# Routed expert blocks in a three-step pipeline: the down product of a block one step after the transposes of its activations, and gathers that leave out padding rows

## The chip, the cores and the metric

The kernel runs on one core of a Trainium2 chip. The core has a matrix engine (TensorE, PE in the profile), a vector engine (DVE), an activation engine (ACT), a general engine (GpSimd, POOL) and a queue engine (SyncE, SP) that here issues transfers only. The metric is the device time of one execution in microseconds; the number compared is the median of several runs.

## The reference, cut to what matters

One layer of a diffusion backbone over 1152 tokens of width 1024. The change touches the mixture of experts at its end, for which the kernel computes, with x the modulated tokens:

```python
scores = sigmoid(x @ w_router)                    # 64 experts
idx = top 8 experts of a token, limited to 4 of 8 groups
w = scores[idx] / sum * 2.5
counts = bincount(flat_e, length=64)
padded = ceil(counts / 128) * 128                 # each expert: whole blocks of 128 rows
# a block: 128 rows, all of one expert e
y_block = (silu(xb @ w_exp_gate[e]) * (xb @ w_exp_up[e])) @ w_exp_down[e]
routed = segment_sum(y_block[dest] * w_sorted, tok)
shared = (silu(x @ w_sh_gate) * (x @ w_sh_up)) @ w_sh_down
out = routed + shared
```

An expert's weights are 1024 x 256 (gate), 1024 x 256 (up) and 256 x 1024 (down) in float32, 1 MB each. How many blocks an expert has is known on the chip only, after the router; each expert has at least one.

## The kernel before, in words

**Blocks.** The expert stage works through blocks of 128 rows: blocks 0 to 8 (NT = 9) are the nine token tiles with the shared expert, blocks 9, 10, ... are the routed blocks, j = 0, 1, ... in the order of the experts. All engines run the same sequence of steps, one step for each block, written as `step(b, p, j)`, with p the parity that picks one of two buffers. The steps of the shared blocks are unrolled in Python, those of the routed blocks are a loop of the chip over pairs (`routed_steps`, L432 to L438) that ends at the block count in `endtab`.

**A block's way.** x rows come into `xg` (two buffers): for shared blocks a plain load that ACT issues (`load_rows`, L636), for routed ones an indirect gather by POOL from `hx_dram` (L583), by token numbers that DVE copies into `gidx` (L1080). PE transposes them, eight 128 x 128 (L827), ACT copies the result rounded to `xT` high (L686), and DVE subtracts to get `xT` low (L1055). Products are made in three passes of rounded parts (`products`, L792): gate/up has 24 matmuls of 512 columns, down has 12. ACT takes the SiLU of the gate half (L699), DVE multiplies with the up half (L1087) into `h_sb`. PE transposes that, two 128 x 128 (L817), ACT and DVE split it into `hTe` high (L683) and low (L1053), and PE makes the down product into banks 4 and 5. ACT copies it into `yb` (two buffers), for routed blocks times the routing weight (L717); POOL adds it into one of two `acc_dram` arrays with an indirect scatter (L602), by the numbers that DVE copies into `sidx` (L1092).

**PE's order in step b:** transposes of h(b), transposes of x(b+2), gate/up of b+1, down of b. **ACT's:** h high (b), x high (b+2), rounding of the gate/up weights of block j+2's expert if it is new (`gate_up_high`, L619, two halves), SiLU (b+1), rounding of the down weights of block j+1's expert if new (`down_high`, L624), y (b). **DVE's:** h low (b), x low (b+2), token numbers for the gather of j+4, low part of the gate/up weights of j+2's expert (`gate_up_low`, L897, two halves), gating product (b+1), numbers for the scatter of j. **POOL's:** gather j+4 (after the transposes of x(b+2)), low part of the down weights of j+1's expert (`down_low`, L565), scatter of j, which waits until the scatter two blocks before has landed.

**Weights.** SP loads an expert's raw weights into one of two slots: gate and up (L444, L445), down (L448). Its loop (from L511) is for one expert x after another: wait until gate/up of the last one have landed and tell ACT (`publish_gu`, L472), wait for `gu_low` of the expert two back, load gate/up; wait for `d_low` of the expert three back, load down; wait until the down weights before have landed and tell ACT (L476). The split weights too have two slots.

**Lists.** While the shared blocks run, the router's choice is ranked, POOL writes 72 small indirect scatters into `list_dram` (L559), block tables (`etab`, `newtab`, `endtab`) are made by small products and DVE operations placed after certain steps, and the finished lists come back over PE (`lists`, L801) ahead of the gate/up product of block 7. A padding entry of the list has the token number T + p, a row that is filled with zeros in `hx_dram` and thrown away in `acc_dram`.

## Time and profile before

| | |
|---|---|
| median of 3 runs | 1976.12 us (1967.53 to 1976.21) |
| the profiled execution | 1980.55 us |
| its span | 1978.8 us |
| PE busy | 1756.0 us (89%) |
| DVE, ACT, POOL busy | 945.0, 851.0, 774.8 us (48%, 43%, 39%) |
| shared blocks and lists | about 680 to 850 us |
| routed loop | about 850 to 1902 us |
| TensorE's granted clock, mean | 0.95 of full speed |
| moved by DMA | 425.84 MB, 215 GB/s over the span |

All rows are of one profiled execution; its own time is 1.8 us above its span. Matmuls are pipelined, so the distance between the starts of two groups says more than the busy time of one. In a row of the timeline the first number is the start, the second the time, x the number of instructions merged, and the bracket the idle time of that engine before it with what ended it. The name `arena` stands for all buffers that are cut from one large tensor.

### The profile page before, as it was taken

What the parts mean: (1) busy time and instruction counts of PE and PEld (TensorE: products, weight loads), DVE (VectorE), ACT (ScalarE), POOL (GpSimd) and SP (SyncE); (2) the same over time, 40 slices, a digit from 0 to 9 for tenths busy, and PEclk for the clock granted to TensorE, in tenths of its full rate; (3) what the DMA queues carried; (4) which work ended last, traced back from release to release, by engine and by line L of the source; (5) the groups of instructions that cost most, each with busy time, mean ns of one, the idle gap of its engine ahead of it and who ended that gap; (6) DMA issues with size and microseconds to landing.
All of it is one profiled execution on the core that took longest, in us unless ns stands there. A gap on an engine that the chain in (4) does not pass through costs nothing.

```text
span 1978.8 us, 29956 instructions
## 1 busy us (share of the span) xinstructions
PE 1756.0 (89%) x8454; PEld 1357.7 (69%) x8455; DVE 945.0 (48%) x1470; ACT 851.0 (43%) x952; POOL 774.8 (39%) x448
## 2 busy tenths in 40 slices
PE   4799999978889877789998999999999989999865
PEld 1667788868545555567777777888777767777642
DVE  5522310267466843245445455534554564445529
ACT  0521012421023431356557657634675676557623
POOL 2220000300100653256546547643564676646630
PEclk9799999987799888799999999999999999999988
DMA  9504531020552342369879989977899799879976
GB/s 330 171 19 163 173 105 35 14 86 1 194 208 91 98 174 65 113 223 343 249 234 356 299 259 355 323 197 216 265 334 286 255 363 327 292 204 345 343 227 275
DMA packets 104861, 425.84 MB, mean 215 GB/s; under 512 B 13244, under 2 KB 31801, under 8 KB 76656
## 3 DMA queue, kind: packets, MB, share of 16 engines
q1 hardware_dynamic: 62128, 279.38, 37.3%
q0 software_dynamic: 38800, 131.69, 25.6%
q10 hardware_dynamic: 3888, 14.16, 2.1%
q8 instruction: 30, 0.49, 0.1%
q14 instruction: 15, 0.12, 0.0%
HBM read 339.94 MB, written 85.25 MB: 215 GB/s over the span
## 4 chain that ended last, share of the span: by engine, by line
PE 51%; DMA 13%; DVE 12%; issue 9%; ACT 8%; another core or an unknown queue 3%; POOL 1%; ACTq 1%; DVEq 1%; SPq 0%; POOLq 0%
PE ps L792 22%; PE ps L1792 10%; DMA raw<-w_exp_up 7%; ACT gu_split L619 6%; PE ps L1923 5%; DMA arena<-hx_dram,arena 3%; PE ps L827 3%; PE ps L1740 3%; DVE gu_split L897 1%; DVE arena L1614 1%; DVE arena L1087 1%; PE ps L817 1%; DMA arena<-pos_sel 1%; PE ps L1765 1%
## 5 line engine op out<-in xcount | busy, mean ns | idle before, releaser
L792 PE MATMUL ps<-gu_split,xT 128*128 (+1 forms) x2736 | 664.3, 398 | 20.8 <-issue 20.6
L792 PEld LDWEIGHTS ps<-gu_split,xT 128*128 128x128 f32 x2736 | 511.9, 190 | 135.1 <-issue 31.6
L565 POOL TENSOR_TENSOR d_split<-raw,d_split (+1 forms) x65 | 303.8, 4674 | 248.8 <-ACT d_split L624 248.7
L792 PE MATMUL ps<-d_split,hTe 128*128 (+1 forms) x1356 | 335.4, 395 | 16.7 <-issue 12.0
L897 DVE TENSOR_TENSOR gu_split<-raw,gu_split (+1 forms) x130 | 292.6, 2292 | 87.1 <-ACT gu_split L619 80.2
L792 PEld LDWEIGHTS ps<-d_split,hTe 128*128 128x128 f32 x1356 | 258.8, 191 | 75.1 <-issue 16.8
L602 POOL DMA_INDIRECT acc_dram<-arena x104 | 202.9, 1951 | 163.5 <-ACT arena L717 143.5
L619 ACT ACTIVATE gu_split<-raw (+1 forms) x130 | 241.9, 1915 | 26.6 <-SPq L472 17.7
L1792 PE MATMUL ps<-hT_split,w_split 128*128 128x512 f32 (+1 forms) x816 | 192.5, 394 | 3.7 <-DVE w_split L1469 3.7
L1055 DVE TENSOR_TENSOR xT<-ps,xT 128x1024 fp32r<-128x1024 f32 x115 | 140.9, 1225 | 114.7 <-ACT xT L686 112.2
L1792 PEld LDWEIGHTS ps<-hT_split,w_split 128*128 128x128 f32 x816 | 152.1, 190 | 41.6 <-issue 6.0
L1053 DVE TENSOR_TENSOR hTe<-ps,hTe 128x256 fp32r<-128x256 f32 x113 | 48.0, 425 | 262.3 <-ACT hTe L683 250.2
L717 ACT ACTIVATE arena<-ps,arena 128x1024 f32<-128x1024 f32 x104 | 116.0, 1115 | 116.3 <-PE ps L792 115.9
L699 ACT ACTIVATE arena<-ps 128x256 f32<-128x256 f32 x114 | 43.6, 383 | 261.2 <-PE ps L792 252.1
L583 POOL DMA_INDIRECT arena<-hx_dram,arena x108 | 123.2, 1141 | 75.5 <-DVE arena L1080 50.1
L1087 DVE TENSOR_TENSOR arena<-ps,arena 128x256 f32<-128x256 f32 x114 | 70.0, 614 | 165.8 <-ACT arena L699 163.5
L559 POOL DMA_INDIRECT list_dram<-arena x72 | 76.0, 1056 | 182.4 <-DVE arena L974 161.4
L686 ACT ACTIVATE xT<-ps 128x1024 fp32r<-128x1024 f32 x115 | 118.2, 1028 | 57.9 <-PE ps L827 32.1
L827 PE MATMUL ps<-const,arena 128*128 128x128 f32 x920 | 125.0, 281 | 19.4 <-DMA arena<-hx_dram,arena 13.3
L624 ACT ACTIVATE d_split<-raw (+1 forms) x65 | 124.6, 1917 | 22.8 <-issue 19.5
L1923 PE MATMUL ps<-arena 128*128 128x512 f32 x288 | 129.5, 604 | 3.2 <-DVE arena L1002 2.6
L827 PEld LDWEIGHTS ps<-const,arena 128*128 128x128 f32 x920 | 107.5, 145 | 21.6 <-issue 21.6
(285 smaller groups left out, 1501.1 us busy)
## 6 DMA issues: line engine op xcount, KB each, us to landing
raw<-w_exp_gate SPq DMA_DIRECT2D x64, 1024.0 KB
raw<-w_exp_up SPq DMA_DIRECT2D x64, 1024.0 KB
raw<-w_exp_down SPq DMA_DIRECT2D x64, 1024.0 KB
arena<-w_ada SPq DMA_DIRECT2D x16, 1024.0 KB, 4.9
arena<-acc_dram SPq DMA_DIRECT2D x18, 512.0 KB, 18.2
arena<-w_ada SPq DMA_DIRECT2D x4, 2048.0 KB, 20.9
w_raw<-w_in SPq DMA_DIRECT2D x16, 512.0 KB, 4.8
acc_dram<-arena POOLq DMA_DIRECT2D x1, 5120.0 KB
```

The source lines that it names most:

```text
L565: tt(d_split(q, 1), raw_d(q), d_split(q, 0).bitcast(F32), ALU.subtract).then_inc(d_low, 1)
L583: pool.indirect_dma_start(out=xg[:, p, :], out_offset=None, in_=hx_dram, in_offset=bass. IndirectOffsetOnAxis(ap=gidx[:, p:p + 1], axis=0) ...
L602: pool.indirect_dma_start(out=acc_dram[p], out_offset=bass.IndirectOffsetOnAxis(ap=sidx[:, p:p + 1], axis=0), in_=yb[:, p, :], in_offset=N ...
L619: a(gu_split(q, 0, half * (GU // 2), GU // 2), raw_gu(q, half), ACT.Copy).then_inc(gu_high, 1)
L624: a(d_split(q, 0), raw_d(q), ACT.Copy).then_inc(d_high, 1)
L686: a(xT[:, p, 0, :].rearrange("p (h x) -> p h x", h=2), ps[:, 0:2, :], ACT.Copy).then_inc(xT_high, 1)
L792: last = mm(dst, lhs(a, j), rhs(b, j), start=(t == 0), stop=(t == len(terms) - 1))
L827: last = pe.transpose(ps[:, c // 4, (c % 4) * P:(c % 4 + 1) * P], xg[:, p, c * P:(c + 1) * P], ident)
L897: last = tt(part(1), raw_gu(q, half), part(0).bitcast(F32), ALU.subtract)
L1055: tt(two(xT[:, p, 1, :]), ps[:, 0:2, :], two(xT[:, p, 0, :].bitcast(F32)), ALU.subtract).then_inc(xT_ready, 1)
L1792: last = mm(dst, lhsT, rhs, start=(t == 0), stop=(t == len(terms) - 1))
L1923: last = mm(ps[:, 2 * (i % 2) + h, :], yT[:, j, tile(i)], w_out[:, j, h * 512:(h + 1) * 512], start=(start and j == chunks[0]), stop=(j == 1))
```

## The change

The steps of PE are put into another order, with the down product a further step back, and the other engines follow:

- PE's step s: gate/up of s, transposes of h(s-1), transposes of x(s+2), down of s-2. ACT's: SiLU (s), h high (s-1), x high (s+2), gate/up rounding of j+2's expert, y (s-2), down rounding of j's expert. DVE's: gating product (s), h low (s-1), x low (s+2), numbers of gather j+4, gate/up low part of j+2's expert, numbers of scatter j-2. POOL's: gather j+4, down low part of j's expert, scatter j-2. A down product's block is thus two behind the gate/up product of its step.
- The shared blocks have a sequence of their own (`shared_step` and the like) with the router's work placed anew; `lists` stands ahead of the gate/up product of block 8. The first two routed blocks are unrolled, the loop begins at pair 1, and behind it stand the last transposes of h and the last two down products, y copies and scatters. There is no gate/up product for a block past the last pair any more.
- The gather has `bounds_check=T - 1, oob_is_err=False`: rows with a number over T - 1 are not read, and `xg` keeps what stood there. `hx_dram` loses its zero rows and the fill of them.
- SP's loop is unchanged but for the fill that it waited for.

```diff
@@ routed_steps
+            for j in range(2):
+                step(NT + j, (NT + j) % 2, j)
             total = routed_blocks(eng)
-            with eng.Fori(0, PAIRS) as i:
+            with eng.Fori(1, PAIRS) as i:
                 with eng.If(2 * i < total):
                     for u in range(2):
                         step(NT + 2 * i + u, (NT + u) % 2, 2 * i + u)
+            return entry(eng, endtab[0:1, 1:2], min_val=E - 2, max_val=NB - 1)
...
@@ phase3_pool
-                pool.indirect_dma_start(out=xg[:, p, :], out_offset=None, in_=hx_dram, in_offset=bass.
-                                        IndirectOffsetOnAxis(ap=gidx[:, p:p + 1], axis=0)).then_inc(xg_in[p], 16)
...
+                pool.indirect_dma_start(out=xg[:, p, :], out_offset=None, in_=hx_dram, in_offset=bass.IndirectOffsetOnAxis(
+                    ap=gidx[:, p:p + 1], axis=0), bounds_check=T - 1, oob_is_err=False).then_inc(xg_in[p], 16)
...
+            for j in range(4):
+                gather(NT + j, (NT + j) % 2, j)
+            for r in range(2):
+                pool.wait_ge(ysh_out[r], 16 * len(range(r, NT, 2)))
+
+            def step(s, p, j):
+                gather(s + 4, p, j + 4)
+                if_new(pool, j, down_low)
+                if not (isinstance(j, int) and j < 2):
+                    scatter(s - 2, p, j - 2)
+
+            last = routed_steps(pool, step)
+            for u in range(2):
+                scatter(NT + last + u, (NT + u) % 2, last + u)
...
@@ phase3_act
+            def step(b, p, j):
+                silu(b, p)
+                h_high(b - 1, 1 - p)
+                x_high(b + 2, p)
+                if_new(act, j + 2, gate_up_high)
+                if isinstance(j, int) and j < 2:
+                    shared_out(b - 2, p)
+                else:
+                    routed_out(b - 2, p, j - 2)
+                if_new(act, j, down_high)
...
@@ phase3_pe
+            def step(b, p, j):
+                gate_up(b, p, j)
+                turn_h(b - 1, 1 - p)
+                turn_x(b + 2, p, j + 2)
+                down(b - 2, p, j - 2)
+
+            pe.wait_ge(y3_used, NT)
+            turn_x(0, 0, -NT)
+            route(NT - 2)
+            turn_x(1, 1, 1 - NT)
+            for b in range(NT):
+                p = b % 2
+                if b == NT - 1:
+                    lists()
+                gate_up(b, p, -1)
+                if b == 0:
+                    rank(1)
+                    transpose_h2(NT - 1)
+                if b == 1:
+                    route(NT - 1)
+                    turn_x(b + 2, p, b + 2 - NT)
+                    pe.wait_ge(logit_out, NT)
+                if b >= 1:
+                    turn_h(b - 1, 1 - p)
+                if b != 1 and b < NT - 2:
+                    turn_x(b + 2, p, b + 2 - NT)
+                if b == NT - 1:
+                    turn_x(NT, 1 - p, 0)
+                if b >= 2:
+                    down(b - 2, p, -1)
+                if b == NT - 1:
+                    turn_x(NT + 1, p, 1)
...
+            last = routed_steps(pe, step)
+            turn_h(NT + last + 1, (NT + 1) % 2)
+            for u in range(2):
+                down(NT + last + u, (NT + u) % 2, last + u)
...
@@ phase3_dve
+            def step(b, p, j):
+                gate(b, p)
+                h_low(b - 1, 1 - p)
+                x_low(b + 2, p)
+                next_gather(p, j + 4)
+                if_new(dve, j + 2, gate_up_low)
+                if not (isinstance(j, int) and j < 2):
+                    next_scatter(p, j - 2)
```

## Rows read from the trace of the kernel before

**Rows 1.** Timeline of PE: the gate/up groups that open and close the routed loop.

```profile
851.22 2.12 PE L792 MATMUL ps<-gu_split,xT 128*128 x5
...
1893.68 1.64 PE L792 MATMUL ps<-gu_split,xT 128*128 x6
```

**Rows 2.** Timeline of two steps, the second with a new expert.

```profile
1152.99 5.74 PE L792 MATMUL ps<-gu_split,xT 128*128 x24
...
1162.30 5.74 PE L792 MATMUL ps<-gu_split,xT 128*128 x24
...
1163.91 3.73 ACT L619 ACTIVATE gu_split<-raw  x2
...
1166.36 4.49 DVE L897 TENSOR_TENSOR gu_split<-raw,gu_split  x2 [1.00 <-ACT gu_split L619]
...
1168.07 0.39 ACT L699 ACTIVATE arena<-ps 128x256 f32<-128x256 f32 x1 [0.43 <-PE ps L792]
...
1171.42 0.44 PE L817 MATMUL ps<-const,arena 128*128 128x128 f32 x2 [0.67 <-DVE arena L1087]
...
1172.67 5.73 PE L792 MATMUL ps<-gu_split,xT 128*128 x24
```

**Rows 3.** What PE waited for from 890 to 1893 us: total, times, longest.

```profile
PE ps L817 <- DVE arena L1087: 39.7, 43, 3.5
PE ps L792 <- issue: 10.9, 14, 0.9
PE ps L827 <- DMA arena<-hx_dram,arena: 4.9, 5, 1.1
```

**Rows 4.** POOL's L565 in three stretches: busy (count), PEclk, DMA share, GB/s.

```profile
1040.50:1103.90 63.40, 23.96 (x5) 1.00 1.02 353
1568.10:1655.30 87.20, 34.27 (x8) 0.98 1.01 363
1815.40:1884.30 68.90, 25.46 (x6) 0.95 1.00 332
```

**Rows 5.** Chain that ended last: the longest weight load in it.

```profile
1445.73 13.06 DMA raw<-w_exp_up
```

**Rows 6.** Groups of the page: busy us, mean ns, idle before and its releaser.

```profile
L565 POOL TENSOR_TENSOR d_split<-raw,d_split (+1 forms) x65 | 303.8, 4674 | 248.8 <-ACT d_split L624 248.7
...
L602 POOL DMA_INDIRECT acc_dram<-arena x104 | 202.9, 1951 | 163.5 <-ACT arena L717 143.5
...
L717 ACT ACTIVATE arena<-ps,arena 128x1024 f32<-128x1024 f32 x104 | 116.0, 1115 | 116.3 <-PE ps L792 115.9
...
L583 POOL DMA_INDIRECT arena<-hx_dram,arena x108 | 123.2, 1141 | 75.5 <-DVE arena L1080 50.1
...
L624 ACT ACTIVATE d_split<-raw (+1 forms) x65 | 124.6, 1917 | 22.8 <-issue 19.5
```

**Rows 7.** Timeline: POOL and DVE beside each other.

```profile
1191.41 4.60 POOL L565 TENSOR_TENSOR d_split<-raw,d_split  x1
...
1195.86 4.51 DVE L897 TENSOR_TENSOR gu_split<-raw,gu_split  x2 [1.07 <-ACT gu_split L619]
1196.18 3.45 POOL L602 DMA_INDIRECT acc_dram<-arena  x1 [0.17 <-issue]
```

**Rows 8.** Chain that ended last: block 11's gather, another in the loop, the last scatter.

```profile
845.20 4.28 DMA arena<-hx_dram,arena
...
909.63 11.87 DMA arena<-hx_dram,arena
...
1904.32 8.34 DMA acc_dram<-arena
```

**Rows 9.** Timeline of PE ahead of the loop: three groups with idle time before them.

```profile
707.22 5.03 PE L792 MATMUL ps<-d_split,hTe 128*128 128x512 f32 x11 [4.27 <-POOL d_split L565]
...
810.86 0.81 PE L801 MATMUL ps<-const,arena 128*128 128x128 f32 x4 [2.43 <-DMA arena<-list_dram,arena]
...
849.60 1.97 PE L827 MATMUL ps<-const,arena 128*128 128x128 f32 x8 [8.43 <-DMA arena<-hx_dram,arena]
```

More of the change, by code:

```diff
@@ L370, in build @@
         list_rows = carve(R2, 11776, 2, P, 2)
[L371 removed]
+        cmp_b = table(NBP, parts=E)
         skip = table(1, parts=E)
@@ L688, in step @@
+            for b in range(2):
+                x_high(b, b)
+                load_rows(b + 2)
+                if b == 0:
                     ln_std(2 * NT - 2, x1[:, (NT - 1) % 2, :])
                     logits_out(NT - 2)
-                if not dyn and b + 4 < NT:
-                    load_rows(b + 4)
-                if not dyn and b == NT - 2:
-                    act.wait_ge(tables_ready, 1)
-                    gate_up_high(1)
-                if dyn or b == NT - 1:
-                    if_new(act, j + 2, gate_up_high)
@@ L731, in phase3_act @@
+            for b in range(NT):
+                shared_step(b, b % 2)
+            last = routed_steps(act, step)
+            h_high(NT + last + 1, (NT + 1) % 2)
+            for u in range(2):
+                routed_out(NT + last + u, (NT + u) % 2, last + u)
             act.wait_ge(moe_done, 1)
@@ new lines, in turn_h, with down @@
+            def turn_h(b, p):
+                pe.wait_ge(h_ready, b + 1)
+                at_least(pe, hT_ready, b)
+                for c in range(2):
+                    last = pe.transpose(ps[:, 6, c * P:(c + 1) * P], h_sb[:, p, c * P:(c + 1) * P], ident)
+                last.then_inc(ht_mm, 1)
+            def down(b, p, j):
+                x, q = expert(j)
+                pe.wait_ge(hT_ready, b + 1)
+                at_least(pe, y_ready, b)
+                pe.wait_ge(d_low, x + 1)
+                v = [d_split(q, s).rearrange("p (c n) -> p c n", c=2) for s in range(2)]
+                for h in range(2):
+                    last = products(ps[:, 4 + h, :], lambda s, c: hTe[:, p, s, c * P:(c + 1) * P],
+                                    lambda s, c: v[s][:, c, h * 512:(h + 1) * 512], 2)
+                last.then_inc(y_mm, 1)
@@ L828, in step @@
                 last.then_inc(x_t, 1)
-                if is_block(b, -2):
-                    route(NT - 2)
-                if not dyn and b == NT - 3:
-                    lists()
-                if dyn or b >= -1:
-                    x, q = expert(j + 1)
-                    pe.wait_ge(xT_ready, b + 2)
-                    pe.wait_ge(gu_low, x + 1)
-                    w = [gu_split(q, s).rearrange("p (t c n) -> p t c n", t=2, c=KD) for s in range(2)]
-                    products(ps[:, 3 - p, :].rearrange("p (t n) -> p t n", t=2),
-                             lambda s, c: xT[:, 1 - p, s, c * P:(c + 1) * P], lambda s, c: w[s][:, :, c, :], KD)\
-                        .then_inc(gu_mm, 1)
@@ L875, in phase3_pe @@
                     mm(ps[0:1, 7, 4 * E:4 * E + NBP], ones[0:E, :], cmp_b, start=True, stop=True).then_inc(blk_mm, 1)
-            routed_steps(pe, step)
+            last = routed_steps(pe, step)
+            turn_h(NT + last + 1, (NT + 1) % 2)
+            for u in range(2):
+                down(NT + last + u, (NT + u) % 2, last + u)
             for i in range(NT):
@@ L1059, in step @@
+            def step(b, p, j):
+                gate(b, p)
+                h_low(b - 1, 1 - p)
+                x_low(b + 2, p)
+                next_gather(p, j + 4)
+                if_new(dve, j + 2, gate_up_low)
+                if not (isinstance(j, int) and j < 2):
+                    next_scatter(p, j - 2)
+            for b in range(NT):
+                shared_step(b, b % 2)
+                if b == 0:
                     place(1)
-                if is_block(b, 1):
+                if b == 1:
@@ L1112, in phase3_dve @@
                     dve.wait_ge(tables_ready, 1)
-            routed_steps(dve, step)
+            last = routed_steps(dve, step)
+            h_low(NT + last + 1, (NT + 1) % 2)
+            for u in range(2):
+                next_scatter((NT + u) % 2, last + u)
             dve.wait_ge(ln2_in, 48)
```

256 lines of the change are left out of this document (121 added, 135 removed).

## The prediction

> **What bounds the kernel now.** I read the page first, then PE's waits inside the routed loop, then the timeline of single steps, then the queues of the slow steps. The loop runs from the gate/up product of block 10 to the one past the last block: 851.22 to 1893.68 us, 1042.5 us for 103 steps [rows 1]. A step with nothing in its way lasts 9.31 us, the distance between two gate/up groups in [rows 2], and PE is then never idle. So 103 x 9.31 = 958.9 us are PE's own work, and 83.6 us are lost. Those 83.6 us are what a new order can win; nothing of it makes a matmul shorter.
>
> Where they are lost is in [rows 2] and [rows 3]. In a step that brings a new expert, ACT rounds the next gate/up weights (L619, 3.73 us) and DVE takes the low part behind it (L897, 4.49 us), both queued ahead of the SiLU (L699) and the gating product (L1087). The gate/up product of this block ends near 1168.0, the SiLU starts at 1168.07, but L1087 has to wait for L897, which runs to 1170.85; PE's transposes of h (L817), released by L1087, start at 1171.42, and the next gate/up at 1172.67 instead of 1171.61. Some such steps lose another 0.9 us right behind, put down to "issue": PE's sequencer had been held at the wait and starts on the next block's expert number only then. Over most of the loop these waits are L817 39.7 us in 43 pieces, issue 10.9 us in 14, and the gathers 4.9 us in 5 [rows 3].
>
> Not all of that is an ordering matter. In three stretches, 219.5 us and 20 steps in all (6, 8 and 6), nearly every step has a new expert (19 L565 in 20 steps), DMA is busy all the time at 332 to 363 GB/s, and the steps lose 219.5 - 20 x 9.31 = 33.3 us [rows 4]. There the chain goes through one weight load after another, the longest 13.06 us [rows 5]: L817 waits for DVE because the weights came late. The other 83 steps lose 83.6 - 33.3 = 50.3 us.
>
> **The change, part by part.** *The order in PE's step.* Now: transposes of h(b), transposes of x(b+2), gate/up(b+1), down(b). Then: gate/up(b), transposes of h(b-1), of x(b+2), down(b-2). The SiLU and gating of block b get a whole step (9.31 us) before PE needs them, instead of the time of one down product; on ACT and DVE they stand first in the step, ahead of L619 and L897. A DVE that is 2.8 us late (1170.85 against 1168.07) no longer reaches PE, and with PE never held there the 0.9 us of issue go too. Counting the engines' new step against 9.31 us: ACT has L619 3.73, L717 1.12, L624 1.92 and some 1.8 us of small copies, 8.6 us; DVE has L897 4.49 and some 2.5 us; both fit. POOL in a step with a new expert has gather 1.14, L565 4.67 and scatter 1.95 [rows 6], 7.8 us plus some 1 us of gaps; it fits as well, but with 3.45 us for a scatter [rows 7] it is 9.3 us and some 0.6 us of gaps, 9.9 us, and falls 0.6 us behind per step of a run, which two steps without a new expert make up. So of the 50.3 us I keep 12: the gathers' 4.9, about 3 for the shorter runs of new experts, and 4 for POOL's lag. Gain 38 us.
>
> *A loop that the change closes.* The down weights of block j's expert are rounded at the end of ACT's step j, one step later against the gate/up weights than now (L624 and L565 stood at j+1, they go to j). SP's program is not changed: it waits for d_low of the expert three back before it publishes the next gate/up weights (L472), and ACT's L619 waits for that. With new experts in every step the round is L619 3.73 + L717 1.12 + L624 1.92 + L565 4.67 = 11.4 us, with hand-overs and SP's two issues about 12.5 us [rows 2, 6]. It bites only when three experts in a row have one block each: with four blocks over three experts there are 9.31 us more and some 6 to spare. That is the three stretches of [rows 4], whose steps already last 219.5 / 20 = 11.0 us, the late ones near 12.3. The first such step of each is covered by about 3.3 us of slack in L717. The other 10 or 11 lose 12.5 - 9.31 = 3.2 us each, 34 us; that takes the place of the 33.3 us. Gain 0: the stretches don't get faster, and behind the waiting SP the load of the next down weights starts later.
>
> *Skipped rows.* 1152 tokens x 8 experts fill 9216 of 104 x 128 = 13312 rows (L602 x104 in [rows 6]), so 31% of each 512 KB gather on average is not read. Of a step's 4.4 MB in a stretch (12.3 us at some 355 GB/s) that is 0.16 MB, 0.45 us. No step ends on it once the loop above sets the pace: 0, up to 20 x 0.45 = 9 us at best. The price of the check on POOL shows in no row. Bounds: nothing below L583's 1.14 us, and not above the 3.45 of a scatter; I take 1.14, the same instruction, and keep 2.3 x 108 = 250 us of POOL time as an end of which only runs of new experts would show a part, some 20 us.
>
> *Scatters go out later.* POOL's L565 of block j now stands ahead of scatter j-2, which was ready about 7 us before. yb has two buffers, and a scatter alone needs 8.34 us to land [rows 8]. From its start to where a late L717 would hold PE's down product there remain about 14 us. That covers 8.34, and the 11.87 us of a gather in a full queue. Cost 0, up to 2 us in ten steps.
>
> Here a rule stands against the change. In [rows 7] the scatter of 1196.18 lasts 3.45 us beside DVE's L897 of 1195.86 (1.95 on the mean), and that L897 starts 1.07 us after its engine was free, as L565 (4.60 us from 1191.41) ends: the two engines take turns. In the new order L565 falls directly ahead of the next step's L897: 4.60 + 4.51 = 9.1 us of every 9.31 us. I take 0.4 us of lag per step of a run, already in the 12 us. The Trainium skill, SBUF — State Buffer, section on the shared port pair, says that a DVE operation with two SBUF inputs and a GpSimd operation that reads SBUF exclude each other for a whole instruction; the trace agrees. By it alone the sum would lose 0.4 us in each of 64 new-expert steps, 26 us.
>
> *Ahead of the loop.* The shared blocks use the same order with its own placement. PE's wait of 4.27 us for the first down weights goes, since down(0) comes two steps later; the 2.43 us for the lists go, since more products stand ahead of them. The wait of 8.43 us for the gather of block 11 goes too (the three waits are in [rows 9]), but POOL now waits for both last shared outputs before it gathers block 13, and these are written in ACT's step of block 10: the gather starts about 1 us after PE wants it, and a gather alone took 4.28 us [rows 8]. With the full queue's 11.87 us as the other end I put 7.5 us in place of 8.43. Together 4.3 + 2.4 + 0.9 = 7.6 us.
>
> *Behind the loop.* The gate/up product for a block that does not exist (5.35 us of [rows 1]'s last step) goes. Two down products now follow each other through one pair of PSUM banks, each waiting for L717 (1.12 us and hand-overs): 2.6 us back. Gain 2.7 us. The smaller hx_dram and the dropped fill are worth nothing; POOL was idle there.
>
> **Sum.** 38 + 0 + 0 + 7.6 + 2.7 = 48 us off the profiled execution's 1980.6 us, 1932 us. That execution lies 4.4 us above the median of the runs shown (1976.12), so the forecast is 1928 us, 2.4% faster.
>
> **Rivals.** (1) *A smaller gain: POOL and DVE in turns, and DMA.* DMA was full in the stretches [rows 4]; at full pace pairs of new experts may fall to POOL's 9.9 us and gathers come later. Of 64 new steps, 45 in pairs or runs at 9.9 instead of 9.31 lose 27 us: 1955. For it: [rows 7]. Against: steps without a new expert are 40 of 104 and give time back.
> (2) *A larger gain.* The skipped rows unload the full queue: 9 us in the stretches and 5 us of gather waits, and L717's slack swallows more of the closed loop, 10 us: 1904. Against: in [rows 5] weights, not gathers, are what is waited for.
> (3) *No gain.* The check makes gathers 2 us longer on POOL (20 us), with rival 1 (27 us): 1975.
> (4) *Slower.* One mechanism: the load of gate/up weights m starts only after the down split of expert m-4, so a pair of steps holds 12.5 us plus the load. At 13.1 us of load it makes 12.8 us per step, hardly anything new. It decides once a load takes over 16 us, because the delayed down load and a scatter now share the queue with it: at 20 us the 20 steps last 16.2 instead of 11.0 us, 104 us more, less the 48: 2032. At 16 us, 14.2 per step, it is 64 - 48, 1992. Against: the longest load of the chain is 13.06 us now, and bytes go down.
>
> **Chances.** No change is what a measurement of this kernel can't tell, within 0.5%, 9.9 us of 1976. The forecast (1905 to 1945) 0.53; rival 1 (1945 to 1966) 0.23; rival 2 (under 1905) 0.09; rival 3 0.07; rival 4 0.08. Faster 0.85, same 0.07, slower 0.08. The range, with the forecast's case and rival 1, and the ends of the unknown costs: 1905 to 1962.
>
> **What would show it.** Right: PE's wait L817 for L1087 gone; steps with a new expert at 9.3 to 9.9 us outside the stretches; in the stretches ACT's L619 released by SP's L472, and that by POOL's L565, with steps of 12 to 12.6 us; the gather wait ahead of the loop moved to block 13's; fewer q0 packets. Wrong: waits of PE on L717 or on gathers in ordinary steps, L583 over 2 us, or stretches slower than 13 us per step.

## The result, and the profile after

The changed kernel takes 1958.64 us (median of 14 runs, 1950.49 to 1962.57), the kernel before beside it 1973.49 us (14 runs, 1963.54 to 1981.47): ratio 0.992, 95% interval 0.9905 to 0.9936. That is 0.8% faster where 2.4% was forecast; the time lies in the range, near its upper end. The two profiled executions differ by more, 1980.55 against 1957.18 us (spans 1978.8 and 1955.3 us), 23.5 us, and their traces account for that difference.

In the changed kernel PE's gate/up and down products are L833, its transposes of h and x L865 and L888. ACT rounds gate/up weights in L628 and down weights in L633, and copies y out in L709. POOL's down low part is L572, its gather L590, its scatter L599. SP issues gate, up and down loads in L452, L453 and L456 and waits for the landing of up weights at L480.

The routed loop's opening and closing gate/up products, from PE's timeline, answer to [rows 1]; the second is that of the last block, which stood at 1884.38 before:

```profile
831.16 5.61 PE L833 MATMUL ps<-gu_split,xT 128*128 x24
...
1851.38 5.62 PE L833 MATMUL ps<-gu_split,xT 128*128 x24
```

What PE waited for inside it, from 831 to 1860 us, answers to [rows 3] (total, times, longest):

```profile
PE ps L833 <- ACT arena L709: 30.4, 12, 4.0
PE ps L888 <- DMA arena<-hx_dram,arena: 16.3, 10, 4.7
```

The 39.7 us in 43 pieces behind DVE's gating product are gone, and so is the issue time behind them. New are 12 waits of the down product for ACT's y.

To compare by blocks, take the same 102 steps (block 10's gate/up to the last block's) and what they last beyond 9.28 us each, which is an undisturbed step in every kernel here. Before: 86.6 us; after: 73.7, of which 7.8 is block 13's gather. Cut into 43 steps in four places around the experts with one block (from blocks 27, 41, 83 and 105, for 10, 12, 14 and 7 steps), and the rest:

| part | before | after | forecast gain | measured |
|---|---|---|---|---|
| ahead of the loop, with block 13's gather inside it | - | - | 7.6 | 9.5 |
| ordinary steps (59) | 36.0 | 5.2 | 38 | 30.8 |
| 43 steps with the stretches | 50.6 | 60.7 | 0 | -10.1 |
| behind the loop | - | - | 2.7 | -6.7 |
| sum | | | 48 | 23.5 |

(Ahead: the loop starts 20.1 us earlier; 2.8 of that is a down product still owed, paid back at the end, and 7.8 is block 13's gather. Behind: from the last gate/up to the end of the span 94.4 us before, 103.9 after, less those 2.8.) The cut of the forecast itself, its 20 steps of [rows 4] against the other 82, says the same: those 20 steps lose 34.0 us before and 43.7 after, the others 52.6 and 22.2 (block 13's gather left out).

Windows of the slow steps in the stretches answer to [rows 4] (the length, then busy and count for PE, PEld, DVE, ACT, POOL, then PEclk, DMA share, GB/s). They are 17 steps picked because they are slow, not the same 20 steps as there; the second lies in a fourth stretch that I had counted as ordinary:

```profile
1035.50:1061.00 25.50, 21.50 (x94) 17.48 (x93) 13.38 (x15) 15.96 (x14) 14.02 (x7) 0.88 0.93 306
1165.30:1213.90 48.60, 41.16 (x186) 33.89 (x185) 23.68 (x28) 30.83 (x28) 34.50 (x14) 0.93 0.93 307
1542.10:1627.90 85.80, 72.87 (x323) 59.48 (x323) 42.10 (x47) 52.77 (x48) 48.68 (x20) 0.92 0.88 285
1799.20:1851.40 52.20, 42.24 (x186) 34.33 (x185) 26.56 (x29) 31.91 (x28) 28.38 (x13) 0.90 0.84 256
```

DMA was full in the stretches before (1.00 to 1.02, 332 to 363 GB/s); now 7 to 16% of its time in these windows is empty while PE waits for weights. In the forecast's own 20 steps, now 63.4, 95.0 and 70.8 us long, its share is 0.96, 0.89 and 0.88. One round of such a stretch, from the timeline of all engines:

```profile
1567.99 0.33 SPq L452 DMA_DIRECT2D raw<-w_exp_gate  x1
1568.05 3.71 ACT L628 ACTIVATE gu_split<-raw  x2 [5.72 <-SPq L480]
...
1570.48 4.49 DVE L962 TENSOR_TENSOR gu_split<-raw,gu_split  x2 [6.83 <-ACT gu_split L628]
1571.67 1.10 ACT L709 ACTIVATE arena<-ps,arena 128x1024 f32<-128x1024 f32 x1
1572.66 1.90 ACT L633 ACTIVATE d_split<-raw  x1
1573.06 4.60 PE L833 MATMUL ps<-d_split,hTe 128*128 x12 [3.99 <-ACT arena L709]
...
1574.93 4.59 POOL L572 TENSOR_TENSOR d_split<-raw,d_split  x1 [5.99 <-ACT d_split L633]
...
1579.68 0.33 SPq L456 DMA_DIRECT2D raw<-w_exp_down  x1
1579.68 1.59 POOL L599 DMA_INDIRECT acc_dram<-arena  x1 [0.16 <-issue]
1581.58 1.04 POOL L590 DMA_INDIRECT arena<-hx_dram,arena  x1 [0.31 <-issue]
1581.83 0.33 SPq L452 DMA_DIRECT2D raw<-w_exp_gate  x1
```

It is to be read from the bottom. The next gate load (1581.83) starts 13.84 us after this one (1567.99). The loop that the forecast described (L628, L709, L633, L572, SP) is there and takes 11.6 us, to 1579.68. But SP then stands another 1.4 us at L480, because the up weights that it asked for at 1568.42 have not landed; they take 13.10 us, to 1581.52. ACT's y copy is queued behind its rounding, which stands for those weights, so the down product waits 3.99 us for L709; it then runs for 4.60 instead of 3.0 us, with a granted clock of 0.50 in the slice 1574 to 1577 below, the lower of TensorE's two levels (1.2 GHz). The chain of waits names the load in four rounds that follow each other:

```profile
1554.71 12.97 DMA raw<-w_exp_up
1568.42 13.10 DMA raw<-w_exp_up
1582.27 12.46 DMA raw<-w_exp_up
1595.47 13.21 DMA raw<-w_exp_up
```

SP itself stands longest for POOL, and for a landing in five shorter waits behind that. Its waits from 1540 to 1640 us:

```profile
SPq L456 <- POOL d_split L572: 72.2, 7, 13.7
SPq L480 <- DMA raw<-w_exp_up: 10.2, 5, 5.8
```

So the two conditions end close together, and taking one of them away leaves the other.

Windows over that round show a hole in the transfers, in the last two columns (DMA share, GB/s):

```profile
1571.00:1574.00 3.00, 0.94 (x4) 0.78 (x5) 3.00 (x2) 3.00 (x3) 0.00 (x0) 0.96 0.98 262
1574.00:1577.00 3.00, 3.00 (x9) 2.35 (x8) 2.75 (x5) 2.03 (x4) 2.07 (x1) 0.50 1.00 380
1577.00:1579.70 2.70, 2.70 (x13) 2.26 (x12) 0.34 (x2) 0.00 (x0) 2.54 (x2) 0.97 0.69 287
1579.70:1582.30 2.60, 2.60 (x14) 2.13 (x13) 0.00 (x0) 0.41 (x1) 2.29 (x2) 1.00 0.62 221
```

From 1577 on little but the tail of one load is left to move: the next down load, the scatter and the gather all stand behind POOL's L572 or behind SP. In the same stretch before, eight slices from 1577.60 to 1599.60 have no share under 0.98, and gate loads follow each other after 11.8 us on the mean (1565.55 to 1648.29, seven gaps).

### The profile page after: what moved, and what is told of

Its sections match the earlier page's. It is cut to its first block, busy times and chain, and to the rows that moved or that the text cites. A ratio compares the mean times of both kernels' runs of the same rounds, so it can differ in the third digit from the quotient of the medians.

```text
span 1955.3 us, 30374 instructions
## 1 busy us (share of the span) xinstructions
PE 1744.1 (89%) x8430; PEld 1363.7 (70%) x8431; DVE 939.1 (48%) x1472; ACT 837.7 (43%) x949; POOL 755.1 (39%) x447
## 3 DMA queue, kind: packets, MB, share of 16 engines
q0 software_dynamic: 38656, 112.31, 23.2%
## 4 chain that ended last, share of the span: by engine, by line
PE 60%; DMA 18%; DVE 10%; issue 6%; ACT 4%; POOL 1%; ACTq 1%; SPq 0%; DVEq 0%; POOLq 0%
PE ps L833 30%; PE ps L1894 11%; DMA raw<-w_exp_up 8%; DMA arena<-hx_dram,arena 6%; PE ps L2025 4%; PE ps L888 4%; PE ps L1842 3%; DMA acc_dram<-arena 2%; DVE arena L1716 1%; POOL d_split L572 1%; PE ps L865 1%; DMA arena<-pos_sel 1%; PE ps L1867 1%; PE ps L1979 1%; PE ps L2018 1%
## 5 line engine op out<-in xcount | busy, mean ns | idle before, releaser
L833 PE MATMUL ps<-gu_split,xT 128*128 (+1 forms) x2712 | 638.6, 391 | 4.1 <-issue 4.1
L833 PEld LDWEIGHTS ps<-gu_split,xT 128*128 128x128 f32 x2712 | 510.7, 189 | 111.0 <-issue 4.6
L833 PE MATMUL ps<-d_split,hTe 128*128 (+1 forms) x1356 | 364.9, 420 | 37.5 <-ACT arena L709 32.3
L572 POOL TENSOR_TENSOR d_split<-raw,d_split (+1 forms) x65 | 299.4, 4607 | 199.5 <-ACT d_split L633 198.5
L962 DVE TENSOR_TENSOR gu_split<-raw,gu_split (+1 forms) x130 | 293.9, 2303 | 135.2 <-ACT gu_split L628 131.2
L833 PEld LDWEIGHTS ps<-d_split,hTe 128*128 128x128 f32 x1356 | 263.4, 201 | 96.6 <-issue 43.5
L628 ACT ACTIVATE gu_split<-raw (+1 forms) x130 | 241.2, 1907 | 74.1 <-SPq L480 63.6
L590 POOL DMA_INDIRECT arena<-hx_dram,arena x108 | 138.0, 1277 | 210.1 <-DVE arena L1133 162.6
L599 POOL DMA_INDIRECT acc_dram<-arena x104 | 171.2, 1646 | 91.9 <-DVE arena L1138 58.9
L709 ACT ACTIVATE arena<-ps,arena 128x1024 f32<-128x1024 f32 x104 | 115.4, 1110 | 120.6 <-PE ps L833 61.0
L888 PE MATMUL ps<-const,arena 128*128 128x128 f32 x920 | 125.0, 280 | 36.8 <-DMA arena<-hx_dram,arena 24.3
L715 ACT ACTIVATE arena<-ps 128x256 f32<-128x256 f32 x113 | 43.1, 381 | 234.4 <-PE ps L833 201.1
L888 PEld LDWEIGHTS ps<-const,arena 128*128 128x128 f32 x920 | 106.5, 144 | 41.9 <-issue 33.4
L633 ACT ACTIVATE d_split<-raw (+1 forms) x65 | 124.0, 1908 | 7.9 <-issue 3.8
L2025 PEld LDWEIGHTS ps<-arena 128*128 128x128 f32 x288 | 54.7, 195 | 64.9 <-issue 62.8
```

The costliest lines, as they stand in the source:

```text
L572: tt(d_split(q, 1), raw_d(q), d_split(q, 0).bitcast(F32), ALU.subtract).then_inc(d_low, 1)
L590: pool.indirect_dma_start(out=xg[:, p, :], out_offset=None, in_=hx_dram, in_offset=bass.IndirectOffsetOnAxis(ap=gidx[:, p:p + 1], axis=0), ...
L599: pool.indirect_dma_start(out=acc_dram[p], out_offset=bass.IndirectOffsetOnAxis(ap=sidx[:, p:p + 1], axis=0), in_=yb[:, p, :], in_offset=N ...
L628: a(gu_split(q, 0, half * (GU // 2), GU // 2), raw_gu(q, half), ACT.Copy).then_inc(gu_high, 1)
L633: a(d_split(q, 0), raw_d(q), ACT.Copy).then_inc(d_high, 1)
L833: last = mm(dst, lhs(a, j), rhs(b, j), start=(t == 0), stop=(t == len(terms) - 1))
```

## The experiments

A line's number differs by a few between kernels. "Excess" is what the last 95 steps to the last block last beyond 9.28 us, in the 43 steps with the stretches and in the other 52; it is of one profiled execution each. The experiments ran on three chips; the kernel before had a median of 1972.56 us on the first, 1952.52 on the second, 1948.82 on the third, so only ratios are compared. The chip of the first measurement isn't on record; with 1973.49 us for the kernel before, it is counted with the first here.

| kernel | chip | ratio (95%) | stretches | other |
|---|---|---|---|---|
| before | - | 1 | 50.6 | 29.6 |
| before, profiled again | 2 | - | 46.4 | 30.9 |
| after | - | 0.992 (0.9905-0.9936) | 60.7 | 5.0 |
| after, again | 3 | 0.9883 (0.986-0.9906) | 59.1 | 5.9 |
| no empty passes | 1 | 0.9903 (0.9867-0.9939) | 57.2 | 5.1 |
| SP's order | 1 | 1.0057 (1.0034-1.0081) | 67.8 | 19.8 |
| shared wait later | 1 | 0.9855 (0.9818-0.9893) | 56.4 | 7.5 |
| before + skipped rows | 1 | 0.9971 (0.9946-0.9996) | 40.9 | 28.6 |
| scatter first | 2 | 0.9871 (0.9847-0.9896) | 59.6 | 0.7 |
| down loads on ACT's queue | 2 | 0.9936 (0.9912-0.996) | 58.4 | 14.1 |
| shared wait + scatter first | 3 | 0.9854 (0.983-0.9877) | 60.2 | 0.7 |
| all three | 2 | 0.9749 (0.972-0.9779) | 43.1 | 6.8 |
| all three, no empty passes | 3 | 0.9725 (0.9702-0.9748) | 42.7 | 9.6 |

**The empty passes behind the loop.** The chip's loop has room for 68 pairs, and 52 are in use. In the profile after, PE stands for 9.26 us between the last gate/up product and the transposes behind the loop:

```profile
1870.10 0.68 PE L865 MATMUL ps<-const,arena 128*128 128x128 f32 x2 [9.26 <-issue]
...
1881.99 1.11 ACT L709 ACTIVATE arena<-ps,arena 128x1024 f32<-128x1024 f32 x1 [5.16 <-PE ps L833]
1883.99 1.56 POOL L599 DMA_INDIRECT acc_dram<-arena  x1 [4.60 <-ACT arena L709]
```

Edit (it leaves out the room for other routings):

```diff
-            with eng.Fori(1, PAIRS) as i:
+            with eng.Fori(1, 52) as i:
```

> The changed kernel with the chip's loop ended after pair 51 instead of 67: these inputs have 104 routed blocks, so the passes left out do nothing. Theory (empty passes): behind the last step PE's transposes of h waited 9.26 us for nothing but 16 passes of an empty loop; without them that wait goes and the time falls by 8 to 9 us, to 0.9955 of the changed kernel. Rival (the last products wait for ACT or for the first-in-first-out of weights): the transposes start as late as before, time within 2 us.

1955.16 us, ratio 0.9903. The 9.26 us of idle time are gone, but the last y copy moved by 1.7 us only (1881.99 to 1880.25), and 1.1 us of that the last gate/up product had already gained. It waits for another thing:

```profile
1869.09 1.59 POOL L599 DMA_INDIRECT acc_dram<-arena  x1 [0.17 <-issue]
...
1880.25 1.11 ACT L709 ACTIVATE arena<-ps,arena 128x1024 f32<-128x1024 f32 x1 [11.72 <-DMA acc_dram<-arena]
```

A scatter that POOL issued behind a down split lands 10.9 us later, and holds the buffer of the last y. The idle time was a cover for it. The gain, 0.17% against the changed kernel's first ratio, is inside the two intervals.

**SP's order.** The loop that the forecast put its stretches on has SP wait for POOL's down split before it publishes the next gate/up weights. This kernel publishes first and loads down weights one expert later:

```diff
+                    sp.wait_ge(d_low, x - 3)
+                    load_down(sp, 1 - q, row("down", x - 3))
+                    publish_d(q, m)
                     sp.wait_ge(gu_low, x - 1)
                     load_gate_up(sp, 1 - q, row("gate", x - 1), row("up", x - 1))
-                    sp.wait_ge(d_low, x - 2)
-                    load_down(sp, q, row("down", x - 2))
-                    publish_d(1 - q, m + q)
```

> The changed kernel with SP's loop put in another order: it announces gate/up of an expert before it waits for the down split of an earlier one, and loads down weights one expert later. Theory (closed loop): in stretches of one-block experts ACT's L628 waited for SP, SP for POOL's L572, 13.3 to 13.8 us per step; this wait goes, steps fall to 12.0 to 12.3 us (DMA full again, share 1.0), and the four stretches together give 15 to 20 us: 1940 us. Rival (DMA is the bound there anyway): steps stay at 13 to 14 us with DMA below 0.95, time within 4 us of the changed kernel.

1985.53 us, ratio 1.0057: slower by 1.4% than the changed kernel. SP's own waits, from 850 to 1900 us, show that the edit did what it says. First the changed kernel, then this one:

```profile
SPq L456 <- POOL d_split L572: 428.7, 52, 15.0
...
SPq L480 <- DMA raw<-w_exp_up: 203.6, 44, 11.1
```

```profile
SPq L480 <- DMA raw<-w_exp_up: 627.3, 58, 14.6
...
SPq L456 <- POOL d_split L584: 23.5, 3, 11.4
```

The wait for POOL is gone and the stretches are no faster (67.8 us of excess for 60.7): gate loads still start 12.5 to 14.6 us apart (1588.67, 1601.20, 1615.77, 1628.32), each when the one before has landed. The later down weights cost in ordinary places as well. So the loop over POOL alone does not set the pace. The run doesn't show what a load takes when it is issued apart, since here SP issues the down load and the gate/up load in one go (1587.91 to 1589.10).

**The wait for the shared outputs.** POOL waits for them ahead of its first routed step, and block 13's gather stands behind that wait:

```profile
847.02 0.99 POOL L590 DMA_INDIRECT arena<-hx_dram,arena  x1 [20.79 <-DMA acc_dram<-arena]
```

```diff
-            for r in range(2):
-                pool.wait_ge(ysh_out[r], 16 * len(range(r, NT, 2)))
             def step(s, p, j):
                 gather(s + 4, p, j + 4)
                 if_new(pool, j, down_low)
                 if not (isinstance(j, int) and j < 2):
                     scatter(s - 2, p, j - 2)
+                elif j == 1:
+                    for r in range(2):
+                        pool.wait_ge(ysh_out[r], 16 * len(range(r, NT, 2)))
```

> The changed kernel with POOL's wait for the shared outputs put behind step 1, right ahead of the first scatter, instead of ahead of step 0's gather. Theory: the gather of block 13 goes out 15 us earlier, the step at 840 us falls from 17.1 to 9.3 us, time falls by 6 to 8 us. Rival (the gather is late since its two-buffer turn or the full queue holds it): the step loses still 4 us or more, time falls by under 3 us.

1946.37 us, ratio 0.9855, 0.65% under the changed kernel. In the trace the 17.10 us step at 840 is 9.3 us long, which is the 7.8 us. The profiled executions differ by 6.6 us; that the medians differ by some 12 is not explained by it. On the third chip that step of the changed kernel lasts 15.80 us, and moving the wait together with the scatter gave 5.0 us of median there (below).

**Skipped rows alone.** The kernel before, with the gather's bound:

```diff
-                                        IndirectOffsetOnAxis(ap=gidx[:, p:p + 1], axis=0)).then_inc(xg_in[p], 16)
+                                        IndirectOffsetOnAxis(ap=gidx[:, p:p + 1], axis=0),
+                                        bounds_check=T - 1, oob_is_err=False).then_inc(xg_in[p], 16)
```

> The kernel before with the skipping of padding rows alone (its fill of zero rows kept). Theory: 19 MB less on q0, and only the DMA-bound stretches get something of it, 0 to 9 us: 1968 to 1973 us. Rival (the check costs POOL time): gathers last over 1.5 us in the mean and the time rises by 5 us or more. Rival (the skip is what the whole change gains): 1958 us.

1966.9 us, ratio 0.9971: 5.7 us, inside the forecast's 0 to 9. The gain stands where the forecast put it: the stretches have 40.9 us of excess for 50.6 and 46.4 in the two profiles of the kernel before, the other steps 28.6 for 29.6 and 30.9. Queue q0, of the gathers and scatters, in the page before and in this run's:

```profile
q0 software_dynamic: 38800, 131.69, 25.6%
...
q0 software_dynamic: 38800, 112.83, 23.7%
```

The packets are as many as before, with 18.9 MB less, which is what 108 gathers of 512 KB hold beyond 9216 rows of 4 KB. The engines' time on it fell from 506.6 to 467.1 us (the share times the span), 8% for 14% of the bytes, and the packets under 512 B rose from 13244 to 17852: a skipped row still costs something. The gather's instruction on POOL takes 1.21 us for the 1.14 of [rows 6], in the changed kernel 1.28. What the skipping gives in the changed kernel no run shows.

**Before, profiled again**, to see how much of a stretch is one execution's chance.

> The kernel before, profiled once more. Its first profile stood 7 us above the median of its runs. If the four stretches of one-block experts carry that difference, their 25 steps last less than the 270.3 us of the first profile while the other steps repeat it within 2 us; if not, the difference lies spread or outside the loop.

1949.39 us on the second chip. The stretches hold 46.4 us of excess and the other steps 30.9, for 50.6 and 29.6 in the first profile. So some 4 us of a stretch sum are one execution's chance. Most of the 31 us between the two executions is from elsewhere (last section).

**The scatter ahead of the down split**, and DVE's scatter numbers ahead of its gate/up low part:

```diff
                 gather(s + 4, p, j + 4)
-                if_new(pool, j, down_low)
                 if not (isinstance(j, int) and j < 2):
                     scatter(s - 2, p, j - 2)
+                if_new(pool, j, down_low)
```

> The changed kernel with POOL's scatter ahead of the split of the down weights, and DVE's scatter numbers ahead of its split of the gate/up weights. Theory (the delayed scatter costs more than I gave it): scatters start within 2 us of L709, the gather behind them comes earlier, PE's gather waits fall from 24 us to under 15, the last two y copies don't wait for a landing; 8 to 15 us less than the changed kernel, 1944 to 1951 us. The stretches keep their 13 to 14 us per step. Rival (scatters were hidden, as I had predicted): within 3 us of it.

1928.42 us, ratio 0.9871. Of PE's waits for gathers (16.3 us above) only block 13's is left, 4.5 us, and the ordinary steps lose next to nothing any more (0.7 us in 52). The two moves were not run apart. In the changed kernel ACT's y copy waits for a scatter's landing, and POOL's scatter for DVE's scatter numbers (58.9 us in 22 from 860 to 1850 us), and neither wait is left here:

```profile
ACT arena L709 <- DMA acc_dram<-arena: 57.0, 23, 4.7
```

Against the changed kernel of the third chip (0.9883) the gain is within the intervals. The stretches have not moved, 59.6 us; six gaps between gate loads in the one at 1500 us are 14.1 to 15.0 us.

**Down weights from ACT's queue.** ACT issues the next down load itself, behind its rounding and once POOL's part of the expert before is done, and SP has gate/up weights alone:

```diff
+                with act.If(nx < E):
+                    act.wait_ge(d_low, nx)
+                    act.dma_start(raw_d(1 - q), A["w_exp_down"][0][bass.ds(nc.s_assert_within(nx, 0, E - 1), 1)].rearrange("o a b -> (o a) b")
+                                  .rearrange("(p j) n -> p (j n)", p=P)).then_inc(d_act, 16)
...
-                    sp.wait_ge(d_low, x - 2)
-                    load_down(sp, q, row("down", x - 2))
-                    publish_d(1 - q, m + q)
```

> The changed kernel with the down weights loaded from ACT's queue, each right behind the rounding of the expert's before, so that SP only loads gate/up weights and waits for no down split. Theory (a closed loop over SP, and a second over the load that is issued behind the same wait): steps of the stretches fall from 13.7 to about 12 us, 15 to 20 us less than the changed kernel, 1939 to 1944 us. Rival (the weights' transfer sets 13 us whatever the order): steps stay at 13 us or more, within 4 us of it. Rival (ACT's load is now late): ACT waits for its own down weights and it gets slower.

1941.29 us, ratio 0.9936: nothing gained, and 0.5% lost against the changed kernel on the third chip. The stretches keep 58.4 us, the other steps go from 5.9 to 14.1. Together with the run of SP's order this shows that without the wait for POOL the landing of the loads paces a stretch: SP's only wait in it is for up weights (96.0 us in 8 between 1540 and 1640), and gate loads start 13.95 and 13.42 us apart (1571.89, 1585.84, 1599.26).

**All three edits.**

> The changed kernel with three edits: the wait for the shared outputs behind step 1, scatter ahead of split, down weights from ACT's queue. If the causes are separate their gains add up, 12 + 8 to 15 + 15 to 20 us: 1912 to 1924 us, 0.970 to 0.975 of the kernel before. If DMA has no more room the sum is cut to 20 us: 1938 us.

1905.91 us, ratio 0.9749: faster than both kernels, 1.4 to 1.7% under the changed one by its two ratios. The excess in the stretches falls to 43.1 us, which no edit did alone. That is less than before the change (50.6 and 46.4) because the 43 steps also hold ordinary ones; in the 20 steps of [rows 4] it is 38.5, for 43.7 and 41.7 in the changed kernel and 34.0 and 28.7 before. So a quarter to a half of what the change cost there comes back. Windows of 1542 to 1556 us, in the same stretch:

```profile
1542.00:1544.00 2.00, 2.00 (x13) 1.68 (x13) 1.50 (x1) 2.00 (x2) 1.84 (x2) 1.00 0.97 332
1544.00:1546.00 2.00, 1.48 (x11) 1.13 (x9) 2.00 (x2) 2.00 (x2) 2.00 (x1) 1.00 1.01 401
...
1548.00:1550.30 2.30, 2.30 (x11) 1.90 (x11) 1.55 (x5) 0.06 (x1) 2.30 (x2) 1.00 1.03 404
1550.30:1553.00 2.70, 2.70 (x13) 2.25 (x12) 0.19 (x1) 2.62 (x2) 2.70 (x1) 1.00 0.94 243
1553.00:1556.00 3.00, 2.37 (x16) 1.88 (x15) 3.00 (x2) 3.00 (x3) 2.84 (x2) 1.00 1.04 310
```

No slice is under 0.94 from 1540 to 1563.7, and the granted clock stays at its upper level (2.4 GHz). They lie in two rounds, of 10.3 and 13.4 us. Over seven rounds, from 1491.26 to 1575.05, gate loads follow each other after 12.0 us on the mean, as before the change (11.8), where the changed kernel takes 13.2 to 13.9 from 1554 to 1609.

**The changed kernel again, and two of the three edits, on one chip.**

> The changed kernel again, unedited, on the chip of the two runs beside it, so that all of them have their stretches and their times beside the same kernel. Against before: 0.992, as in the first measurement, within its interval. In the stretches with one block to an expert the same 13 to 14 us to a step, if they come from the order of the waits; near 11, as in the second profile of before, if the first chip alone was slow.

1926.22 us, ratio 0.9883. Steps of the stretch at 1541 last 13.1, 15.5, 11.4 and 15.2 us, so the slow rounds are not one chip's. The gain of the change is thus 0.8% in the first measurement and 1.2% in this one; the difference between them is not explained.

> The wait for the shared outputs moved behind POOL's step 1 and the scatter ahead of the down split, without the down weights on ACT's queue. Theory: the down weights behind POOL's split on SP's queue are what keeps the DMA engines idle in the stretches, and ACT's queue pays only once the scatter is early (alone it gave nothing: 0.9936). The two edits alone gave 0.9855 and 0.9871 against 0.992, so 0.6 and 0.5 per cent: added up 0.9806, and the kernel with all three, 0.9749, is then 0.5 per cent faster than this one for its stretches. Rival: the down weights' queue is nothing here either, and the two edits help each other: 0.975 to 0.977.

1921.23 us, ratio 0.9854: 0.3% under the changed kernel on the same chip, inside the two intervals, and the step from here to all three edits is 1.05%, clear of them. The stretches keep 60.2 us of excess, and fall to 43.1 with the third edit. The theory had 0.9806 for this kernel and the rival 0.975 to 0.977, and both are wrong in size: the two edits give less together than apart, and the down weights' queue gives about twice what I had for it. But the theory's mechanism is what the windows show. The end of one round:

```profile
1533.80:1540.00 6.20, 1.57 (x7) 1.15 (x6) 3.74 (x2) 6.17 (x4) 0.62 (x2) 0.86 0.98 391
1540.00:1544.00 4.00, 4.00 (x16) 3.21 (x15) 2.89 (x6) 1.80 (x4) 4.00 (x2) 0.78 0.85 242
1544.00:1547.80 3.80, 3.80 (x19) 3.14 (x18) 0.00 (x0) 0.00 (x0) 3.64 (x2) 1.00 0.48 93
```

With the scatter early but the down load still behind POOL's split on SP's queue, DMA is half empty for the last 3.8 us of a round. With the down load free but the scatter late (down weights from ACT's queue), there is a hole as well:

```profile
1572.30:1574.00 1.70, 1.70 (x13) 1.34 (x11) 0.00 (x0) 1.70 (x2) 1.03 (x1) 1.00 0.64 116
```

Only with both edits did the rounds get shorter. Why the rounds with the down load free alone took 13.4 to 14.0 us at a DMA share of 0.90 (over 1567.3 to 1609) isn't settled.

Two orders that bear on a round were never run. In every kernel SP waits for a gate/up load to land before it issues the next, though the slot was free in the round above once L962 had ended at 1574.97, and the next load started at 1581.83. And ACT's y copy, for which PE waits 30.4 us, stayed behind ACT's rounding of gate/up weights. What either would give isn't shown.

**All three, without the empty passes.**

> All three edits and the chip's loop ended at the last block in use, as the first experiment did for the changed kernel. That one gave 0.2 per cent with 9.26 us of idle time gone, because the last output waited for the landing of the scatter before it, which POOL had issued behind a down split. With the scatter ahead of the split that wait should be gone: 7 to 9 us under the kernel with three edits, so 0.970 to 0.972. Rival: the scatters' landings (6 us each for the last ones) set the end whatever the passes do: 1 to 3 us, 0.9735.

1894.99 us, ratio 0.9725, the lowest here, though inside the interval of the kernel with the passes. From the last gate/up product to the end of the span it needs 101.2 us, with the passes 104.1: 2.9 us less, the rival's size, where 9.3 us of idle time are gone (by the ratios 0.24%, 4.7 us, with each kernel on another chip). The rest came back as waits for POOL, whose last down splits stand behind the scatters now:

```profile
1816.15 4.61 PE L836 MATMUL ps<-d_split,hTe 128*128 x12 [3.83 <-POOL d_split L566]
...
1823.81 4.47 PE L836 MATMUL ps<-d_split,hTe 128*128 x12 [3.05 <-POOL d_split L566]
```

## Why the prediction was right and wrong

**The order in PE's step: right.** The waits for the gating product and the issue time behind them are gone, steps with a new expert last 9.3 us, and 30.8 us come back in the ordinary steps of my cut for 38 forecast (30.4 by the forecast's own cut). Part of the missing 7 us is the fourth stretch, which the forecast counted as ordinary and which got slower (8.4 to 11.6 us of excess in its 12 steps). Taken together, the loop gives 20.7 us.

**A loop that the change closes: wrong, and the largest error.** "Gain 0: the stretches don't get faster" was 10.1 us lost (12.7 in the second pair of profiles, the kernel before on the second chip and the changed one on the third), and in exactly the forecast's 20 steps 9.7 (13.0). The step that failed is the round of 12.5 us. In its place the runs show rounds of 13.2 to 13.9 us (gate loads from 1554.28 to 1608.98). The sum behind the 12.5 held: 11.4 us forecast, 11.6 measured to SP's down load. What I left out is that a second condition ended last in five rounds of the stretch, the landing of the gate/up load, 13.5 us after the gate load's issue in the round above. A load of 13.06 us stood in [rows 5] and in rival 4, but I did not put it against the 12.5 us in the forecast itself. It was misread as well: it starts at 1445.73, in none of the three stretches, whose loads took 10.1 to 12.9 us in the chain before. So the landing is no fixed price. The change puts the down load, the scatter and the gather behind the same split of POOL, and DMA idles at the end of a round and is crowded at its start. Two runs that remove SP's wait for POOL leave the rounds at 12.5 to 14.6 us; with the scatter early as well they fall to 12.0 on the mean. That the burst itself makes a load land later is argued from the windows and from that pair of edits, and the rest of the loss stays open.

**Skipped rows: inside the bounds** of 0 to 9 us, 5.7 measured, but in the kernel before; the 0 was for the changed kernel, where nothing tests it. Of the sign "fewer q0 packets" next to nothing came (38656 for 38800); the bytes fell, from 131.69 to 112.31 MB.

**Scatters go out later: wrong.** "Cost 0, up to 2 us in ten steps": the y copies wait 57.0 us in 23 pieces for a landing, which the sum of 14 us had ruled out; with the scatter (and DVE's numbers for it) early, all gather waits but block 13's and 4 of the last 5 us of excess in ordinary steps vanish; the last y waits 11.72 us for a late scatter once the cover is away, and with the scatter early the stretches can be mended at all. In the time, scatter first alone is worth 0.1 to 0.5%.

**POOL and DVE in turns: the rule held, the cost did not come.** In the round above L572 starts at 1574.93 as L962 ends at 1574.97. In a pair of rows that do overlap, the later one is longer by about as much: L572 runs from 1196.47 to 1201.10, L962 starts at 1199.89 and lasts 5.57 instead of 4.49 us. The Trainium skill, SBUF — State Buffer, section SBUF: two separate sides, says of the shared port pair that one instruction holds it to its end while the other blocks, and the trace agrees. With the scatter beside DVE's low part (scatter first) its mean is 2.20 us, against 1.65 (L599) in the changed kernel. But the lag of 0.4 us per step of a run shows nowhere: the changed kernel's order puts the scatter behind L572, where it takes 1.59 us, and POOL has time over: L572 waits 188.2 us in 52 pieces for ACT's rounding. Rival 1 has nearly the measured time (1955 for 1958.64 us), for another reason; that the time lies in the range is luck to that extent.

**Ahead of the loop: the number near, its terms only in part.** It is 9.5 us for 7.6, and block 13's gather costs 7.8 us for 7.5. The 4.27 us for the first down weights are gone. But in the first profile a wait of 7.99 us for a gather still stands at 815.35, so the 8.43 us did not go, and both first profiles hold single matmuls with nothing waited for (last section). In the second pair of profiles, which has none, the wait for the lists is 15.1 us before and 18.2 after, where the forecast had it gone, and the part gives 5.5 us (14.8 earlier, less 2.8 and 6.5). The nearness of 9.5 to 7.6 is luck in part.

**Behind the loop: wrong in sign.** I counted a product that goes and a PSUM pair that is shared, 2.7 us gained; 6.7 were lost. The last transposes of h and two down products now stand behind the loop's empty passes (9.26 us), which the sum had no term for; before, PE had nothing left to do but wait for the last scatter [rows 8]. With that gap closed, a scatter behind a down split took its place, and the time behind the last gate/up product fell by 0.5 us only.

**Rivals 2 to 4.** Skipped rows unloaded the queue, but the stretches got slower; the check costs 0.07 to 0.14 us a gather, not 2; and no weight load in the changed kernel's chain took 16 us (13.21 at most), so the loop of rival 4 wasn't reached, though its kind of wait, a load's landing, ends most rounds. Of the signs of being wrong, stretches slower than 13 us per step came, and waits for gathers in ordinary steps, most of them under 2 us.

## What to carry to other kernels

When a step is moved behind a long instruction of another engine, list the transfers that are thereby issued together. Here work for DMA that was spread over a step became a burst and a hole, and a stretch that DMA had bounded got longer though no byte was added. Where several waits could end a round, write the time of each beside the others, the transfer's landing among them, and don't stop at the loop that looks closed. Of two edits that each left a hole, neither shortened the rounds; test such edits together before dropping either.

## What was not expected of the hardware

In the first measurement PE issued single matmuls 0.7 to 2.1 us apart for some 20 us ahead of the loop, and again for some 16 us later, with nothing waited for. The kernel before shows the same there, from 730 and from 786 us. From the timeline of the changed kernel's first profile:

```profile
726.30 0.39 PE L833 MATMUL ps<-d_split,hTe 128*128 128x512 f32 x1 [1.70 <-issue]
727.70 0.59 PE L833 MATMUL ps<-d_split,hTe 128*128 128x512 f32 x1 [1.00 <-issue]
...
736.83 0.21 PE L791 MATMUL ps<-arena 128*128 128x64 bf16 x1 [1.89 <-issue]
738.23 0.21 PE L791 MATMUL ps<-arena 128*128 128x64 bf16 x1 [1.20 <-issue]
```

In its profile on the third chip the same work takes one piece with no issue time there, and what PE waits for in its place is the lists, 18.2 us:

```profile
PE ps L842 <- DMA arena<-list_dram,arena: 18.2, 1, 18.2
```

Block 17's step, where the count of 95 begins, starts at 904.04 us in the one and at 877.87 in the other, 26 us apart, while the loop behind it takes the same time within 1 us. The kernel before differs likewise between its two profiles, 922.63 and 893.15. What PE's sequencer stood for isn't in the trace.

An empty pass of the chip's loop costs PE about 0.58 us (9.26 us for 16). A scatter of 128 rows of 4 KB that takes 8.34 us to land in [rows 8] takes 10.9 us in the run without empty passes, when DMA is full from 1872 to 1880 us (share 1.00 and 1.06), and the last one in the changed kernel 6.1 us, at a share of 0.58.
